# Joint attention of a two-layer block: the values of a pair of heads in two halves, and the first scores ahead of the last head transposes

## The reference

```
for l in range(2):
    fx, gx, qx, kx, vx, ax = branches(hx, ..., rope)      # 512 tokens, 8 heads, 96 dims of q and k, 64 of v
    fy, gy, qy, ky, vy, ay = branches(hy, ..., None)      # 256 context tokens
    ox = softmax(qx @ [ky, kx].T * 96**-0.5) @ [vy, vx] * silu(ax)    # keys of both: 768
    x  = x + gate * (concat([fx, gx, ox]) @ w_out[l])
    if l == 0:                                            # the context is updated in layer 0 only
        oy = softmax(qy @ ky.T * 96**-0.5) @ vy * silu(ay)            # 256 keys
        y  = y + gate_c * (concat([fy, gy, oy]) @ w_out[l])
```

## Time and profile before

| what | us |
|---|---|
| median of 3 runs | 2172.76 (2172.22 to 2173.36) |
| profiled execution | 2174.57 |
| its span in the trace | 2173.2 |
| PE busy in the span | 2145.1 (99%) |
| DVE, ACT, POOL busy | 997.2, 799.3, 734.5 |
| joint attention, layer 0 | about 1691 to 1813 |
| joint attention, layer 1 | about 2031 to 2132 |

### The profile page before, as it was taken

One profiled execution on the slowest core, in us unless ns is written; L12 is line 12 of the kernel. 1 busy time (PEld: TensorE's weight loads), 2 busy tenths in 40 slices (PEclk: granted clock), 3 DMA queues, 4 the chain that ended last, 5 costly groups with the idle time before them and its releaser, 6 DMA issues.

```text
span 2173.2 us, 30673 instructions
## 1 busy us (share of the span) xinstructions
PE 2145.1 (99%) x12586; PEld 1754.2 (81%) x12586; DVE 997.2 (46%) x1764; ACT 799.3 (37%) x1371; POOL 734.5 (34%) x339
## 2 busy tenths in 40 slices
PE   9999999999999999999999999999999999999999
PEld 8778888888889898888878888887886667886677
DVE  5664555541222333334465555345305673552672
ACT  6445333333333333334443333333225442334531
POOL 3116444455443333333174444443221002232102
PEclk9999999999999999999999999999999999999999
DMA  4103444432322222221034444322110001322002
GB/s 153 40 30 110 145 145 146 144 126 97 107 93 88 82 81 82 78 88 69 35 121 146 145 146 146 135 97 95 59 68 35 1 1 40 110 78 83 1 2 78
DMA packets 57659, 191.53 MB, mean 88 GB/s; under 512 B 8112, under 2 KB 11440, under 8 KB 57264
## 3 DMA queue, kind: packets, MB, share of 16 engines
q1 hardware_dynamic: 46128, 155.82, 20.6%
q10 hardware_dynamic: 11392, 33.75, 4.4%
HBM read 185.35 MB, written 2.10 MB: 86 GB/s over the span
## 4 chain that ended last, share of the span: by engine, by line
PE 88%; DVE 3%; ACT 1%; issue 1%; DVEq 1%; POOL 0%; ACTq 0%; POOLq 0%; DMA 0%
PE ps L180 21%; PE ps L181 21%; PE ps L182 21%; PE ps L2729 4%; PE ps L183 3%; PE ps L185 3%; PE ps L184 3%; PE ps L2761 2%; PE ps L2741 2%; PE ps L1105 2%; PE ps L1139 1%; PE ps L1121 1%; PE ps L2284 0%; PE ps L2250 0%; PE ps L2097 0%
## 5 line engine op out<-in xcount | busy, mean ns | idle before, releaser
L253 POOL TENSOR_TENSOR w_lo<-w_raw,w_hi 128x1024 fp32r<-128x1024 f32 x282 | 682.0, 2419 | 1332.2 <-ACT w_hi L170 1318.0
L170 ACT ACTIVATE w_hi<-w_raw 128x1024 fp32r<-128x1024 f32 x284 | 300.3, 1058 | 539.3 <-DMA w_raw<-in_wstream 539.0
L180 PE MATMUL ps<-h_hi,w_hi 128*128 128x512 f32 x1168 | 464.0, 397 | 2.7 <-DVE w_lo L295 1.8
L182 PE MATMUL ps<-h_hi,w_lo 128*128 128x512 f32 x1168 | 455.0, 390 | 0.0
L181 PE MATMUL ps<-h_lo,w_hi 128*128 128x512 f32 x1168 | 455.0, 390 | 0.0
L180 PEld LDWEIGHTS ps<-h_hi,w_hi 128*128 128x128 f32 x1168 | 219.3, 188 | 50.7 <-DVE w_lo L295 2.0
L182 PEld LDWEIGHTS ps<-h_hi,w_lo 128*128 128x128 f32 x1168 | 219.3, 188 | 46.0
L181 PEld LDWEIGHTS ps<-h_lo,w_hi 128*128 128x128 f32 x1168 | 219.5, 188 | 43.3 <-issue 0.7
L183 PE MATMUL ps<-w_hi,h_hi 128*128 128x256 f32 x416 | 116.6, 280 | 0.0
L185 PE MATMUL ps<-w_hi,h_lo 128*128 128x256 f32 x416 | 115.5, 278 | 0.0
L184 PE MATMUL ps<-w_lo,h_hi 128*128 128x256 f32 x416 | 115.5, 278 | 0.0
(11 more groups left out here) (362 smaller groups left out, 4019.5 us busy)
## 6 DMA issues: line engine op xcount, KB each, us to landing
w_raw<-in_wstream SPq DMA_DIRECT2D x283, 512.0 KB, 3.2
f0mod_rows<-in_wmod ACTq DMA_DIRECT2D x24, 512.0 KB, 4.6
f1mod_rows<-in_wmod ACTq DMA_DIRECT2D x24, 512.0 KB, 4.6
dvS<-dvE SPq DMA_DIRECT2D x64, 32.0 KB, 2.5
out<-x SPq DMA_DIRECT2D x8, 256.0 KB, 3.2
x<-in_x SPq DMA_DIRECT2D x3, 512.0 KB, 6.9
l_dft<-in_dft ACTq DMA_DIRECT2D x4, 384.0 KB, 4.2
l_wuq<-in_wuq ACTq DMA_DIRECT2D x2, 768.0 KB, 6.1
```

The lines of the kernel that those rows point to most:

```text
L170: self.A.activation(self.slot(self.w_hi, n), self.slot(self.w_raw, n), ACT.Copy).then_inc(self.w_high, 1)
L180: T.matmul(out, wh, ah, start=start, stop=False)
L182: return T.matmul(out, wl, ah, start=False, stop=stop)
L253: G.tensor_tensor(c.slot(c.w_lo, n), c.slot(c.w_raw, n), c.slot(c.w_hi, n).bitcast(F32), ALU.subtract).then_inc(c.w_low, 1)
```

## The change

Three edits. First, in the heads, `scores(0)` is issued a transpose group earlier in both layers: in layer 0 in turn nj + 1 after a wait for one evacuation fewer, with `scores(1)` behind the last transposes; in layer 1 `scores(0)` ahead of the transposes of job nj - 2 and `scores(1)` ahead of those of the last job. Second, in a step of the joint attention PE turns first and sums afterwards, and the values of a pair of singles are cut in two: key tiles 0 to 2 in the step in which all twelve came before, tiles 3 to 5 a step later. Third, the tables move: the gating of a tile whose last unit is a single, and in layer 1 its spreading, come one step later, and the norm never ahead of the gate.

```diff
-            if i == self.nj + 1:
-
+            if i >= self.nj:
+                s = i - self.nj
                 if self.turn_bank(self.nj - 1) == self.job_bank(self.nj - 1):
-                    T.wait_ge(e.copied_out.h, self.co0 + self.nj - 2)
-                else:
-                    T.wait_ge(e.evacuated.h, self.ev0 + self.nj)
-                self.joint.scores(0)
-                self.joint.scores(1)
+                    T.wait_ge(e.copied_out.h, self.co0 + self.nj - 3 + s)
+                    self.joint.scores(s)
+                elif s:
+                    T.wait_ge(e.evacuated.h, self.ev0 + self.nj - 1)
+                    self.joint.scores(0)
...
+        if self.turn_bank(self.nj - 1) != self.job_bank(self.nj - 1):
+            self.joint.scores(1)
...
             if not self.both:
-                self.spreads[self.last[b] + (3 if b < TT - 1 else 2)] = (b, 7)
+                self.spreads[self.last[b] + (4 if b < TT - 1 else 3)] = (b, 7)
...
+            gate = self.last[b] + (4 if self.units[self.last[b]][2] == 1 else 3)
             norm = step + (1 if step >= n or not self.both else 0)
+            norm = max(norm, gate)
             self.inverts.setdefault(step - 1, []).append(b)
-            self.gates.setdefault(self.last[b] + 3, []).append(b)
+            self.gates.setdefault(gate, []).append(b)
...
             if i == self.n + 1:
                 self.y.out_begin(0, 2, 4)
-            if 3 <= i < self.n + 3 and i - 3 in self.of_sum:
-                self.sum_values(i - 3)
             if 2 <= i < self.n + 2:
                 self.turn_probs(i - 2)
+            if i - 4 in self.of_sum and self.units[i - 4][2] == 1:
+                self.sum_values(i - 4, NT // 2, NT)
+            if i - 3 in self.of_sum:
+                self.sum_values(i - 3, 0, NT // 2 if self.units[i - 3][2] == 1 else 2)
...
-    def sum_values(self, i):
+    def sum_values(self, i, k0, k1):
...
-        if pair == 0:
+        if pair == 0 and k0 == 0:
...
-        for k in range(n):
+        for k in range(k0, k1):
...
-        ins.then_inc(e.summed_v.h, 1)
+        if k1 == n:
+            ins.then_inc(e.summed_v.h, 1)
```

## The result

| | before | after |
|---|---|---|
| median, us | 2172.77 (2172.22 to 2173.64, 6 runs) | 2183.65 (2183.21 to 2187.53, 6 runs) |
| profiled execution, us | 2174.57 | 2183.34 |
| ratio | | 1.0053 (95%: 1.0040 to 1.0066) |

The change makes the kernel 10.9 us slower. Slower was forecast, 5.7 us of it, and the time lies 1.4 us above the range. The two profiled executions differ by 8.8 us; the rest is taken up under "The end of the heads".

The account below looks back on a forecast made before the run. PE's own chain of work was taken to bound the kernel. On the 2172.8 us median, -4.1 + 2.8 + 1.8 - .6 + 4.3 + 1.5 = +5.7 gave 2178.5 us, range 2173.0 to 2182.3.

Parts of the forecast that it names:

- The end of the heads: Start of both layers' joint attention: filled waits and full clock save 2.6 us in layer 0, 1.5 in layer 1, together -4.1.
- The steps: Joint attention steps: more value groups at about .29 us each cost +2.8 in layer 1 and +1.8 in layer 0.
- the way back to scores: PE's change from a value group to the scores behind it: taken as .13 us, bounds 0 and .25.
- roomier: Layer 1 steps in which a tile ends: more room on DVE afterwards, taken at -.4 us.
- [T]he .5 stays, now ahead of the transposes: Layer 0, the double's step: PE's wait of about .5 us for DVE's copy stays the same size.
- Does the even length buy anything?: Layer 1 steps: values in every step gain nothing; the copy waiting for the second half is hidden by .1 us.
- The ends: End of the joint attention: -.6 us in layer 0; +4.3 in layer 1 from lost cover, +1.5 for the clock.
- The switch is not free: Rival 1, chance .12: the switch between transposes or scores and halves costs nothing, giving 2171.5 us.
- the clock did not fall at the starts: Rival 2, chance .09: the clock still falls at both layers' starts, +1.6 and +1.5, giving 2181.6 us.
- the end was not cheaper: Rival 3, chance .14: layer 1's end is cheaper, no clock fall (-1.5) and half the copy's wait (-.5), 2176.5 us.
- layer 0 kept its gap: Rival 4, chance .09: layer 0's steps lose their gap, 8 x .5 us less, giving 2174.5 us.

Follow-up runs that it names:

- e2: The changed kernel with its first edit undone, both first scores together as before: 2186.92 us, ratio 1.0069.
- e1: The kernel before with the first edit alone, first scores ahead of the last head transposes: 2170.04 us, ratio 0.9993.
- e12: e1 plus layer 0's double values two steps later and the output projection's first two parts issued ahead of step n's PE work: 2164.43 us, ratio 0.9961.
- e4: e1 with the transposes of a step ahead of the values, values of a pair undivided: 2176.69 us, ratio 1.0021.
- e5: e1 with each pair's values cut into two halves around the transposes of the same step: 2179.38 us, ratio 1.0032.
- e11: The changed kernel with DVE's copy cut to 512 columns, result stale; single run, only steps read: layer 0's 101.28 us became 99.47.
- e3: The changed kernel with the last pair of layer 1 summed whole, its spreading, gate and norm where they were before: 2180.35 us, ratio 1.0038.
- e7: The changed kernel with 24 unread identity transposes on PE in the wait at the end of layer 1: 2182.48 us, ratio 1.0048.

## Why the prediction was right or wrong

**The end of the heads: right in the trace, too large for a median.** The third scores of layer 0 came 2.5 us earlier against what went ahead, layer 1's first transposes of probabilities 1.4 (forecast 2.6 and 1.5), at the full clock, behind waits of 1.0 and .7 + 1.1 (the text said 1.1 and .8 + 1.1). Timeline of PE after the change, against the earlier trace rows, and the two stretches, against the earlier trace rows:

```profile
1690.24 1.08 PE L2284 MATMUL ps<-ident,l_work 128*96 128x128 f32 x8 [1.01 <-DVE l_work L2385]
1691.15 2.75 PE L2735 MATMUL ps<-l_kT,l_qT 96*128 96x512 f32 x8
```

```profile
1690.00:1695.00 5.00, 4.54 (x23) 3.22 (x24) 3.07 (x5) 3.95 (x8) 0.00 (x0) 1.00 0.00 0
2029.50:2036.00 6.50, 4.76 (x24) 3.14 (x25) 2.80 (x4) 4.93 (x7) 2.68 (x5) 1.00 0.00 0
```

None of the eleven traces that have the new heads shows a slow clock at either start; of the two with the old heads, before has it at both and e2 at one.

But most of these 4 us is the clock's fall (a stretch of 3.4 us at half rate gives up 1.7), and the profiled execution of before had it at both starts. e2 shows that layer 1's may not come; layer 1 then gains nothing. The median of e1 shows 2.1. The forecast took differences from one execution, noted that this one lay 1.8 above the median, and did not ask whether its slow stretches were the reason.

They very probably were. The timed runs keep no record of where the clock fell, but they keep its mean. In the sessions of e1 to e12, every run of the kernel before that took up to 2171.2 us has a mean clock of .999, and every one from 2171.7 on has .998: the spread goes with the clock, as it would if the number of slow stretches made it. At equal mean clock, .999, before takes 2170.4 to 2171.2 and e1 2169.6 to 2170.1, only .9 less, which is what layer 0's 2.5 us leave without the clock. So before's profiled execution, with three slow stretches, stood for a slower run than the median, and differences taken from it are too favourable to the change by about one of them. That is the reading of 8.8 us in the traces and 10.9 in the medians. It is not shown run by run.

**The steps: the step of the prediction that failed.** It priced a group in its new place at .29 and said of the way back to scores, "I take the .13 of the transposes behind one, with 0 and .25 as ends". It is .20: the 1.49 above, the same in e4, e5 and e11. A group between transposes and scores costs .35. For layer 1, 13.5 pairs of steps at .35 are 4.7 for the 3.2 forecast. Of that .9 comes back and not .4, and .7 of the .9 for another reason than the "roomier" tile ends: the 27 steps held 14 whole sums before and hold 27 halves now, so half a sum of 1.46 has left the stretch, behind the last scores (e3 finds it there). In layer 0 four groups are .24 dearer in five steps, and a second term was missed. "[T]he .5 stays, now ahead of the transposes" holds for DVE, whose copy ends as late as ever; but PE goes on .04 behind the copy into values and .14 behind it into transposes. The chain before a group of values in e1, and before the transposes in e4:

```profile
1712.78 0.96 DVE j_probT L2815
1713.74 0.04 issue
1713.78 1.53 PE ps L2763 x24
```

```profile
1713.73 0.96 DVE j_probT L2815
1714.69 0.14 issue
1714.83 0.85 PE ps L2743 x6
```

Values behind scores let the wait and the change of width run at the same time; transposes behind scores wait first, and the change comes later as a piece of its own. With .24 and .10 the period is 13.81 + .34 = 14.15; measured 14.21. Seven of them are 2.4 of the 2.65 that layer 0 was off. What inside PE makes the way back to scores dearer than the way back to transposes is not shown.

**Does the even length buy anything?** As forecast, nothing: e11 finds no wait in layer 1's steps, and the copy that waits for the second half is hidden.

**The ends: right.** Layer 0 -.8 for -.6. Layer 1 +4.8 for +4.3. The chain after the change, against the earlier trace rows:

```profile
2131.11 0.88 PE ps L2767 x12
...
2134.94 0.44 PE ps L2781 x4
2135.37 0.83 PE ps L2767 x12
...
2136.23 0.70 DVE rows L2828
...
2137.02 0.70 DVE rows L2845
...
2137.75 0.64 ACT l_m_hi L2877
...
2138.41 0.70 DVE l_m_lo L2850
```

The four of the chain that had run under twelve matmuls stand bare, 3.1 us of them, and the clock falls behind, 1.6 for 1.5. e3 corrects the reason for a part: 3.5 of the 4.8 is the lost cover, 1.3 is work and groups that now fall behind the last scores. e7 confirms the clock.

**The rivals.** None was it. The switch is not free (e5), the clock did not fall at the starts, the end was not cheaper, layer 0 kept its gap. The time is 5.2 us above the forecast: 3.65 are the steps, .6 the other terms of the account, 2.1 the difference between the traces and the medians, less the 1.1 of the unchanged code. With the way back at .20 alone the forecast would have been 3.8 higher and the time inside its range. The range failed because it held the price of the way back from 0 to .25 as one uncertainty of some 2 us, while 64 groups at .06 more, and the wait that no longer overlaps, are more than 4.

## What to carry to other kernels

Count the changes of PE between full-width and 64-column work, and price each neighbour pair by itself: cutting a group in two, to make steps equally long, buys nothing where PE waits for nobody and pays a whole change for each cut. A wait should end at the instruction that has a fixed cost of its own to pay meanwhile, and independent work (here the first parts of the next projection) belongs ahead of a wait, not behind it. Before taking a gain from one trace, ask which of it is a half-rate stretch that another execution may not have.

## What the runs showed of the hardware

- From full-width work into a group of 64-column pairs and back costs .15 + .13 us into transposes and .15 + .20 into scores, whatever the group's length (6 pairs in e5, 12 in e4).
- PE goes on .04 us after the copy it waits for into 64-column values, .14 us into full-width transposes (e1, e4).
- TensorE fell from 2.4 to 1.2 GHz for 3.4 us behind waits of 1.8 to 3.1 us, but by no means behind each. Behind 3.1 us it fell in three traces of three, behind 1.8 at the start of layer 0 in two of two, behind 2.0 at the start of layer 1 in one of two (before, not e2). At two places in the code that all 13 kernels share, it fell in 9 of 13 behind a wait of 2.2 us (at 1490 us) and in 8 of 13 behind one of 2.0 to 2.4 (at 1090). With the wait of 3.1 filled with transposes it stayed at 2.4 GHz (e7).
